# A mixed prompt-and-sample decoder step: the last sampled unit's values in the key buffers, loaded by SyncE

## The reference

```python
def attend_a_sample(q, k, v):                    # dilated window attention, 8 heads x 64
    kk = jnp.concatenate([cwk.astype(k.dtype), k], 1)
    vv = jnp.concatenate([cwv.astype(v.dtype), v], 1)
    o = dilated_mix(q, kk, vv, L + jnp.arange(DS, dtype=jnp.int32))
    ...

def attend_b_sample(q, k, v, lam_):              # differential attention, 4 heads, value of 128
    pk = ck[page_table].reshape(DB, P, N_HEADS_B, 2, HEAD_DIM).astype(k.dtype)
    pv = cv[page_table].reshape(DB, P, N_HEADS_B, 2 * HEAD_DIM).astype(v.dtype)
    kk = jnp.concatenate([pk, k], 1)
    vv = jnp.concatenate([pv, v], 1)
    ...
    return diff_core(q, kk, vv, mask, lam_)

def diff_core(q, k, v, mask, lam):
    s = jnp.einsum('bqhcd,bkhcd->bhcqk', q, k).astype(jnp.float32)
    s = jnp.where(mask, s, -jnp.inf)
    p = jax.nn.softmax(s, axis=-1)
    a = (p[:, :, 0] - lam * p[:, :, 1]).astype(v.dtype)
    return jnp.einsum('bhqk,bkhe->bqhe', a, v)
```

## Time and profile before

| what | us |
|---|---|
| median of 3 runs | 1206.15 |
| lowest and highest run | 1203.51, 1208.47 |
| profiled execution, its own time | 1210.44 |
| span of the profile in that execution | 1208.7 |
| PE busy | 1049.2 (87%) |
| DVE busy | 817.2 (68%) |
| POOL busy | 462.9 (38%) |
| ACT busy | 271.1 (22%) |

### The profile page before, as it was taken

How to read it: one execution, slowest core, us unless ns; L and a number is a source line. 1 busy time by engine, 2 the same in 40 slices (tenths; PEclk the granted TensorE clock), 3 DMA queues, 4 the chain that set the end, 5 groups by cost and what they waited for, 6 DMA issues and landing times.

```text
span 1208.7 us, 24024 instructions
## 1 busy us (share of the span) xinstructions
PE 1049.2 (87%) x9389; PEld 846.9 (70%) x9389; DVE 817.2 (68%) x1485; ACT 271.1 (22%) x600; POOL 462.9 (38%) x587
## 2 busy tenths in 40 slices
PE   4699899985888889878857987999999999999993
PEld 2377567764666556556556767999999999776772
DVE  1637445707878778877557576566757677998868
ACT  0300000011433333334323014223232232101001
POOL 0423224312344434443443006456556565433323
PEclk9699999996989999899957996999999999999997
DMA  8948999869899999999751034556786621413102
GB/s 294 405 144 304 343 334 355 306 213 347 289 337 363 369 310 349 348 364 309 255 202 47 36 96 139 209 209 217 258 287 245 244 70 70 153 58 130 63 3 79
DMA packets 100261, 276.54 MB, mean 229 GB/s; under 512 B 9608, under 2 KB 33174, under 8 KB 96549
## 3 DMA queue, kind: packets, MB, share of 16 engines
q1 hardware_dynamic: 83973, 220.42, 51.8%
q0 software_dynamic: 16128, 54.54, 13.0%
q10 hardware_dynamic: 48, 0.05, 0.0%
HBM read 264.60 MB, written 76.69 MB: 282 GB/s over the span
## 4 chain that ended last, share of the span: by engine, by line
PE 56%; DVE 16%; DMA 10%; issue 8%; SPq 5%; POOL 3%; POOLq 1%; ACT 0%; ACTq 0%; DVEq 0%; PEldq 0%
PE wide L1656 16%; PE wide L1657 15%; PE wide L1658 15%; DMA ring<-in_cache_k 4%; DVE ring L1211 3%; PE wide L1792 3%; DMA ring<-in_w_ada 2%; DMA room<-in_w_ada 2%; SPq L615 2%; DMA ring<-in_w_down 1%; PE wide L1604 1%; SPq L458 1%; DVE ring_r L1135 1%; PE wide L1725 1%; PE wide L1736 1%
## 5 line engine op out<-in xcount | busy, mean ns | idle before, releaser
L787 POOL TENSOR_TENSOR ring_r<-ring,ring_r 128x1024 fp32r<-128x1024 f32 x70 | 183.5, 2629 | 225.8 <-DVE ring_r L1095 205.1
L1656 PE MATMUL wide<-x_sb_r,ring_r 128*128 128x288 f32 x704 | 211.2, 300 | 10.6 <-DVE ht_r L1117 7.5
L1657 PE MATMUL wide<-ht_r,ring_r 128*128 128x288 f32 x704 | 209.4, 297 | 0.0
L1658 PE MATMUL wide<-x_sb_r,ring_r 128*128 128x288 f32 x704 | 208.6, 296 | 0.0
L1658 PE MATMUL wide<-ring_r,ht_r 128*128 128x512 f32 (+1 forms) x400 | 159.0, 398 | 0.0
L1656 PEld LDWEIGHTS wide<-x_sb_r,ring_r 128*128 128x128 f32 x704 | 133.5, 190 | 13.6 <-issue 13.6
L1211 DVE STREAM_TRANSPOSE ring<-ring 128x512 f32<-128x512 f32 x208 | 129.1, 677 | 15.5 <-DMA ring<-in_cache_k 14.8
L1658 PEld LDWEIGHTS wide<-x_sb_r,ring_r 128*128 128x128 f32 x704 | 134.2, 191 | 0.0
L1657 PEld LDWEIGHTS wide<-ht_r,ring_r 128*128 128x128 f32 x704 | 133.9, 190 | 0.0
L1656 PE MATMUL wide<-ring_r,x_sb_r 128*128 128x512 f32 (+1 forms) x240 | 97.8, 407 | 8.8 <-DVE ht_r L1117 8.4
L1657 PE MATMUL wide<-ring_r,x_sb_r 128*128 128x512 f32 (+1 forms) x240 | 95.2, 397 | 0.0
(11 more groups left out here) (239 smaller groups left out, 1977.8 us busy)
## 6 DMA issues: line engine op xcount, KB each, us to landing
ring<-in_cache_k SPq DMA_DIRECT2D x128, 256.0 KB
out_wks<-in_cache_win_k SPq DMA_DIRECT2D x8, 4080.0 KB, 19.0
out_wvs<-in_cache_win_v SPq DMA_DIRECT2D x8, 4080.0 KB, 19.8
ring<-in_w_up SPq DMA_DIRECT2D x22, 1024.0 KB, 7.3
room<-in_w_ada SPq DMA_DIRECT2D x8, 2048.0 KB, 10.2
ring<-in_cache_win_k SPq DMA_DIRECT2D x16, 1024.0 KB
room<-in_cache_v POOLq DMA_DIRECT2D x64, 256.0 KB, 5.7
x_sb<-in_cache_v POOLq DMA_DIRECT2D x64, 256.0 KB, 5.1
```

Of the source, the lines that this page charges most:

```text
L787: nc.gpsimd.tensor_tensor(rest, w, high.bitcast(F32), ALU.subtract).then_inc(wl_rest, 1)
L1656: nc.tensor.matmul(out, left[0], right[0], start=first, stop=False)
L1657: nc.tensor.matmul(out, left[0], right[1], start=False, stop=False)
L1658: return nc.tensor.matmul(out, left[1], right[0], start=False, stop=last)
```

## The change

For groups 1, 2 and 3 of unit 15 the place, the issuer, the wait and the semaphore differ. The place is the key buffer `kraw[G % 3]`; SyncE issues, behind the last keys; it waits until the keys of the same G are transposed; and the arrival is counted in the key buffer's semaphore. TensorE waits for that count and reads from there. `w_o`, which overwrites the key buffers, waits for the last weighing also. Group 0 of the unit stays with GpSimd.

```diff
+        LAST = 2 * DB - 1
+
+        def v_home(w, g):
+
+            G = NG[w] + g
+            if w == LAST and g >= 1:
+                return kraw[G % NK].rearrange("p t d -> p (t d)").rearrange("p (i d) -> p i d", i=4)
+            return vg[G % NV]
+
+        def v_in(w, g):
+
+            return kg_in[(NG[w] + g) % NK] if w == LAST and g >= 1 else vg_in[(NG[w] + g) % NV]
+
         def load_values(eng, w, g):
...
-            vs = G % NV
-            if G >= NV:
+            home, landed = v_home(w, g), v_in(w, g)
+            if w == LAST and g >= 1:
+                eng.wait_ge(kg_t, G + 1)
+            elif G >= NV:
                 eng.wait_ge(sa_vg, G - NV + 1)
...
                 for t, pg in enumerate(page_numbers(eng, b, g)):
-                    eng.dma_start(vg[vs][t:P:4, :, :],
+                    eng.dma_start(home[t:P:4, :, :],
                                   flat_v[1][bass.ds(pg, 1)].rearrange("a (i m) h d -> m (a i) (h d)", i=4))\
-                        .then_inc(vg_in[vs], 16)
+                        .then_inc(landed, 16)
...
                 elif here:
                     load_key_tail(sp, w)
+            for g in range(1, 4):
+                load_values(sp, LAST, g)
             sp.wait_ge(sa_pv, len(sa) - 1)
             load_new_values(sp, len(sa) - 1)
...
             sp.wait_ge(sa_g, NG[len(sa)])
+            sp.wait_ge(sa_vg, NG[len(sa)])
             for n in range(FIRST_LATE, FIRST_LATE + 2):
                 load_chunk(n)
...
-                    load_values(pool, w, g)
+                    if w < LAST or g == 0:
+                        load_values(pool, w, g)
...
-                pe.wait_ge(vg_in[G % NV], v_count(m, w, g))
+                pe.wait_ge(v_in(w, g), k_count(m, w, g) + 64 if w == LAST and g >= 1 else v_count(m, w, g))
...
-                                                vg[G % NV][:, i, P * j:P * j + P], start=(g == 0 and i == 0),
+                                                v_home(w, g)[:, i, P * j:P * j + P], start=(g == 0 and i == 0),
```

More of the change, by code:

```diff
@@ L471, in load_values @@
                 for t in range(4):
-                    eng.dma_start(vg[vs][t:P:4, :, :],
-                                  win_v[:, 4 * g + t, :].rearrange("(i m) f -> m i f", i=4)).then_inc(vg_in[vs], 16)
+                    eng.dma_start(home[t:P:4, :, :],
+                                  win_v[:, 4 * g + t, :].rearrange("(i m) f -> m i f", i=4)).then_inc(landed, 16)
             elif m == 0:
                 for t in range(2):
-                    eng.dma_start(vg[vs][t:P:4, :, :],
-                                  win_v[96:128, 8 + 4 * t:12 + 4 * t, :]).then_inc(vg_in[vs], 32)
+                    eng.dma_start(home[t:P:4, :, :],
+                                  win_v[96:128, 8 + 4 * t:12 + 4 * t, :]).then_inc(landed, 32)
             else:
                 for t, pg in enumerate(page_numbers(eng, b, g)):
-                    eng.dma_start(vg[vs][t:P:4, :, :],
+                    eng.dma_start(home[t:P:4, :, :],
                                   flat_v[1][bass.ds(pg, 1)].rearrange("a (i m) h d -> m (a i) (h d)", i=4))\
-                        .then_inc(vg_in[vs], 16)
+                        .then_inc(landed, 16)
         @block.sync
```

## The result

| | before | after | ratio, 95% interval |
|---|---|---|---|
| first occasion, median us (runs) | 1207.55 (7) | 1195.27 (7) | 0.9898 (0.9878 to 0.9919) |
| second occasion, median us (runs) | 1208.77 (11) | 1193.34 (6) | 0.9866 (0.9840 to 0.9892) |
| the profiled execution, its own time | 1210.44 | 1195.27 | |
| its span | 1208.7 | 1193.5 | |

The change makes the kernel faster by 1.0 to 1.3%, 12 to 15 us; 1194 was forecast, with 1188 to 1201 as the range.

A forecast was written before the change was run, and what follows sets the result against it. It took TensorE's 9.3 us of waits for value loads in unit 15's weighing as the bound; five steps carried their removal to gates 12.5 us earlier, which off the median 1206.15 gives 1193.7, forecast 1194, range 1188 to 1201.

The forecast's parts named there:

- Step 1: Weighing of unit 15: four groups back to back, ending at 602.5 instead of 613.73, 11.2 us earlier.
- Step 2: Row sums behind the weighing: 1.7 us at 2.4 GHz instead of 3.2, ending at 604.2, 12.7 us earlier.
- Step 3: VectorE's output scaling without GpSimd beside it: 2.45 and 1.23 us, ending at 608.8 instead of 627.3.
- Step 4: w_o's load goes out later, at 602.6; first half lands in 8.4 us, second 5.5 later; only 5 us gained.
- Step 5: GpSimd's w_o split slows VectorE's splits, one operation per piece; gates at 641.9, 12.5 us earlier.
- (a): Rival at w_o's load: its first half needs 15.3 us and bounds; gain only 5.5 us, 1200.6; chance 0.12.
- (b): Rival at unit 14: moved loads share the engines and delay its values 4 us; gain 8.5, 1197.7; chance 0.12.
- (c): Rival at VectorE's splits: two operations per GpSimd piece, splits end at 636; gain 16.5, 1189.7; chance 0.08.
- (d): Rival at SyncE's value loads: groups land slowly, 10 us or more each; 6 us slower, 1212; chance 0.04.
- (e): Rival: clock stays at 1.2 GHz through the gates, or group 0 is late; gain eaten up, 1204; chance 0.02.

The follow-up runs named there:

- wo_late_only: The kernel before with one wait more, w_o also waiting for the last weighing; ratio 0.9930 to the kernel before.
- wo_half_early: The changed kernel with other homes for groups 1 to 3, so w_o's first half goes out behind the value loads; 0.9891 of the kernel before.
- defer_after: The changed kernel with GpSimd's last four pieces of w_o's split waiting for VectorE's eight splits of transposed rows; 0.9815 of the kernel before.
- place_only: The changed kernel with GpSimd instead of SyncE issuing the three groups into the key buffers, w_o still late; 0.9872 of the kernel before.

## Why the prediction was right

**Step 1, the end of weighing.** 11.2 us were forecast; from first to last weighing it is 15.1 less 3.7, 11.4. The bytes were in by about 592, the early end of the 592 to 595 forecast. What the prediction did not see is how the hole came about: it named both the pace of the four buffers and w_o's traffic, and the sum needed only their total. The last piece, at 606.06, it put down to the buffers. But three pieces of the same group had gone from 599.31 on the earlier trace rows, and a group waits for its buffer once, ahead of its first piece; the 5.03 us before the fourth were no wait for a buffer. `wo_late_only` takes away w_o's part alone, the pause falls to 1.43 us, and 6.3 us of the weighing come back.

**Step 2, the sums.** 1.7 us at 2.4 GHz forecast; 1.8 measured (601.4 to 603.22), the granted clock at 1.00.

**Step 3, the scalings.** 2.45 and 1.23 forecast, 2.29 and 1.23 measured.

**Step 4, w_o.** 8.4 us forecast for the first half, 8.0 measured; 5.5 more for the second, 4.9 measured (12.9). The Trainium skill's fit for GpSimd's DMAs ("DMA: Bandwidth & Descriptors", section "Anatomy of one DMA") would have 6.8 us for 2 MB, an estimate; the trace does not agree for this load of SyncE's, which had the second half right behind it, and the measurement decides. ScalarE was done with the first transposes at 615.37, forecast 616.9, of which 0.9 is the earlier start.

**Step 5, the collision, is the term that was mis-sized.** Forecast: GpSimd without a gap from 612.1 to 634.7, seven VectorE operations beside it, splits done at 640.0 and the gates at 641.9. Measured: 610.68 to 631.09, seven operations beside it (the small one, three casts, three subtractions), splits done at 637.28 and the gates at 638.44. The form held; the price of a piece was taken too high. It took 2.55 us and not 2.8 (22.6 over eight): I had taken the middle between the two batches of the earlier trace rows, and the dearer of them, 12.32 us, had run beside the scalings, which met no piece this time. That is 2.2 us. TensorE came 1.2 us behind the splits instead of 1.9: the row at 637.04 is 0.41 us, the price at 2.4 GHz. With the 0.9 us of the earlier start and 0.4 of w_o's landing that is 4.2 us. Against it stands what VectorE had left when GpSimd was through: six splits had been done beside it, where seven were forecast, and the last of them ended 0.55 us behind the last piece, so that the rest took 6.2 us (631.09 to 637.28) and not 5.3. The difference to explain is 3.5 us, 641.9 to 638.44.

So the stretch gave 15.1 us instead of 12.5. The medians of the first runs moved by 12.3, those of the second by 15.4. By the intervals the gain is 9.8 to 14.7 us on the first occasion and 13.1 to 19.3 on the second, so each of the two numbers lies outside one of them, and the runs cannot tell 12.5 from 15.1. That 1194 lies between the two medians (1195.27 and 1193.34) is in part luck: the mechanism held, but the profile's 15.1 us off the same median would be 1191.

**The rivals.** (a) w_o as the bound: its first half landed in 8.0 us, not 15.3, and `wo_half_early` shows that even the 5.9 us for which ScalarE stood are worth nothing. (b) Unit 14 delayed: its weighings at 587.18 and 588.07 begin without a wait. The loads of its kind (line 487, 560 to 630 us) took 4.1, 5.4 and 7.2 us from issue to landing (least, median, most), where the earlier trace rows had 3.6, 5.2 and 6.8: no doubling, though the engines were full (362 GB/s from 580 to 584, 396 from 584 to 588). TensorE did lose something there: it stood 2.64 us for VectorE ahead of 578.38, the granted clock of 580 to 584 is 0.69, and from 578.38 to unit 15's first weighing it took 19.4 us, where from the same row of before (580.85) it took 17.8. That stand began at 575.7, before the first moved load went out at 576.15, and `defer_after`, which has the same loads, took 17.8 us. The Trainium skill, "DMA: Bandwidth & Descriptors", section "Queues, rings and completion order", has the engines go round-robin between queues; that the moved loads then take half of each engine was the prediction's inference. No run here shows that sharing itself, and if it took place it cost nothing. (c) Less collision: one operation per piece, not two. Yet its time came close: it had the gates "at 638 or before" and 16.5 us of gain, and measured were 638.44, with the unit 0.9 us early, and 15.1; what brought the time there was the cheaper piece, not its mechanism. (d) Slow loads on SyncE's queue: 6.7 us at most from issue to landing. (e) did not happen: group 0 was weighed without a wait, and the clock, 1.2 GHz from 612 to 636, was at 2.4 at the gates.

**What was wrong in the reasoning, though not in the number.** The title of the change speaks of SyncE as the issuer, and the prediction took that for a needed part (SyncE has "some 17 us to read page numbers and issue", GpSimd a pause of 5.5 us). `place_only` shows that it is not: GpSimd's long pause went away with w_o's bytes, and without them GpSimd is quick enough.

## What to carry to other kernels

A large weight load that is released early is not free: look at what else is in the DMA engines between its release and its first use, and hold it back if the stage ends on one of those other loads. Where one engine slows another operation by operation, moving the work earlier only moves the collision; what gained here was to give the less urgent half a wait, so that it starts when the other engine is through with its urgent operations. And an experiment that separates a change into its parts is worth its run even where the forecast was right: about half of this gain was to be had with one line (0.9930, with 0.9866 for the whole change).

## What was not expected of the hardware

GpSimd's fill of 128x1024 hardly slows VectorE: beside four fills (618.99 to 623.75) the casts took 0.53 us instead of 0.42 and the subtractions 0.69 as ever, while GpSimd's tensor_tensor of that size made the same operations take 2.6 and 2.7. Which of two GpSimd operations runs beside VectorE thus made VectorE's operations four to five times as long.
